# Forming the first modulation's shift and scale inside the input product's stage

## The reference, cut to what matters

```python
c_act = jax.nn.silu(c)                                   # c: (1, 1024)
mod = c_act @ w_ada[l] + b_ada[l]                        # w_ada: (1024, 6*1024)
shift1, scale1, gate1, shift2, scale2, gate2 = jnp.split(mod, 6)
h = layer_norm(x) * (1.0 + scale1) + shift1              # x: (1024, 1024)
proj = h @ w_in[l]                                       # w_in: (1024, 6416)
```

## Time and profile before

| | |
|---|---|
| Median of 3 runs | 4945.96 us (4945.6 to 4948.31) |
| The profiled execution's own time | 4957.9 us |
| Its span in the trace | 4956.0 us |
| PE busy | 4270.7 us (86%) |
| DVE, ACT, POOL busy | 53%, 31%, 15% |
| Moved by DMA | 589.38 MB, mean 119 GB/s |

### The profile page before, as it was taken

The page is one execution under the profiler, slowest core; times in us unless marked ns, Lnnn a source line. Parts: engine busy times, 40 slices in busy tenths (PEclk is TensorE's granted clock), DMA queues, the critical chain, the costliest instruction groups (busy, mean ns, idle before and its releaser), DMA issues. The chain is left out here.

```text
span 4956.0 us, 70950 instructions
## 1 busy us (share of the span) xinstructions
PE 4270.7 (86%) x27114; PEld 3547.5 (72%) x27114; DVE 2633.8 (53%) x4845; ACT 1526.3 (31%) x3235; POOL 741.6 (15%) x796
## 2 busy tenths in 40 slices
PE   5999999866999999699967576999985799989978
PEld 3899888555788877599966133888874699965646
DVE  3557774655343358411107696777754425546745
ACT  3233221633222235211114242334433411133423
POOL 1111111221000000000004012111112114423321
PEclk8999999777999999799988588999986899999998
DMA  4544432531211144322121484434424335543334
GB/s 158 165 141 139 146 127 78 195 138 60 59 51 42 34 153 166 102 86 86 65 107 49 165 299 158 105 98 112 108 65 132 124 106 173 182 147 101 100 98 136
DMA packets 430680, 589.38 MB, mean 119 GB/s; under 512 B 166297, under 2 KB 317201, under 8 KB 428771
## 3 DMA queue, kind: packets, MB, share of 16 engines
q1 hardware_dynamic: 382425, 418.41, 27.6%
q0 software_dynamic: 46336, 164.57, 8.9%
q10 hardware_dynamic: 1616, 2.36, 0.1%
HBM read 429.67 MB, written 155.57 MB: 118 GB/s over the span
## 5 line engine op out<-in xcount | busy, mean ns | idle before, releaser
L320 PE MATMUL g_in_g_acc<-g_in_g_whi,g_in_hi 128*128 128x444 f32 (+4 forms) x960 | 357.0, 372 | 16.6 <-DVE g_in_g_wlo L310 9.9
L321 PE MATMUL g_in_g_acc<-g_in_g_wlo,g_in_hi 128*128 128x444 f32 (+4 forms) x960 | 346.3, 361 | 0.0
L322 PE MATMUL g_in_g_acc<-g_in_g_whi,g_in_lo 128*128 128x444 f32 (+4 forms) x960 | 345.7, 360 | 0.0
L196 PE MATMUL g_even_acc<-g_even_w_hi,h_hi 128*128 128x384 f32 (+1 forms) x960 | 317.3, 331 | 19.5 <-DVE g_even_w_lo L238 19.5
L198 PE MATMUL g_even_acc<-g_even_w_lo,h_hi 128*128 128x384 f32 (+1 forms) x960 | 317.1, 330 | 0.0
L199 PE MATMUL g_even_acc<-g_even_w_hi,h_lo 128*128 128x384 f32 (+1 forms) x960 | 317.1, 330 | 0.0
L320 PE MATMUL g_odd_g_acc<-g_odd_g_whi,h_hi 128*128 128x344 f32 (+3 forms) x816 | 263.9, 323 | 31.9 <-DVE g_odd_g_wlo L310 16.8
L321 PE MATMUL g_odd_g_acc<-g_odd_g_wlo,h_hi 128*128 128x344 f32 (+3 forms) x816 | 261.8, 321 | 0.0
L322 PE MATMUL g_odd_g_acc<-g_odd_g_whi,h_lo 128*128 128x344 f32 (+3 forms) x816 | 261.7, 321 | 0.0
L1597 DVE SCALAR_TENSOR_TENSOR up_cv<-up_acc,up_taps,up_cv 128x1023 f32<-128x1023 f32 x88 | 112.8, 1282 | 279.7 <-ACT up_cv L1573 272.5
L214 DVE COPY g_even_o_buf<-g_even_acc 128x384 f32<-128x384 f32 (+1 forms) x60 | 32.1, 535 | 399.2 <-PE g_even_acc L199 399.2
(11 more groups left out here) (582 smaller groups left out, 10357.3 us busy)
## 6 DMA issues: line engine op xcount, KB each, us to landing
down_raw<-in_w_down SPq DMA_DIRECT2D x66, 512.0 KB
g_in_m_w<-in_ada_w SPq DMA_DIRECT2D x24, 1024.0 KB, 5.7
up_w_buf<-in_w_up SPq DMA_DIRECT2D x44, 512.0 KB
U2p<-g_even_o_buf POOLq DMA_DIRECT2D x11, 1920.0 KB, 7.8
g_odd_x<-U3p SPq DMA_DIRECT2D x24, 768.0 KB
g_even_w_buf<-in_even_w_in SPq DMA_DIRECT2D x11, 1536.0 KB
g_in_m_w<-in_w_ada SPq DMA_DIRECT2D x16, 1024.0 KB, 6.1
prep_near<-U2p SPq DMA_DIRECT2D x18, 896.0 KB
```

What stands on the lines that cost most here:

```text
L196: mm = pe.matmul(o, hi[:, k, tt], w_hi[:, par, k, :wd], start=k == 0, stop=not split and k == kc - 1)
L320: pe.matmul(bank[:, :wd], hi[:, k, tt], w_hi[:, st % 2, k, :wd], start=k == 0, stop=False)
L321: pe.matmul(bank[:, :wd], hi[:, k, tt], w_lo[:, st % 2, k, :wd], start=False, stop=False)
L322: op = pe.matmul(bank[:, :wd], lo[:, k, tt], w_hi[:, st % 2, k, :wd], start=False, stop=k == KC - 1)
```

## The change

`start_stage` and `ada_stage` go. `in_stage` takes their work:

- The first weights are loaded by SP at the head of its queue into `first_w`, in 8 transfers of 1 MB (four strips of 512 columns, each in two halves), with the loads of the first four chunks of `w_in` between the second and the third strip. `first_w` lies in the memory that `hi` and `lo` take later.
- ACT issues the loads of `c`, of the bias as 16 rows and of `ident`, takes silu, and issues the four writes of zero rows. The first reader of the padded tensors' stage is guarded by `pad_out` in `load_x`.
- PE transposes the bias rows (into `bias_T`), then forms the modulation as columns: the weights are the stationary operand (128 rows by 64 columns), one column of `c_first` is the moving one, and the two halves of 64 columns go to partitions 0 to 63 and 64 to 127. That is 64 such products for a strip, 256 in all: strips 0 and 1 ahead of the transposes of block 0, strips 2 and 3 behind them.
- DVE copies the turned bias to `cols` ahead of norm(0), and adds the sums to it in turn_in(0).

```diff
+FIRST = 4
-        start_stage(nc, ident, T["t_eye"], (U2p, U3p))
-        ada_stage(nc, [([T["c"][0]], T["w_ada"][0][:, 0:2 * D], T["b_ada"][0][0:2 * D], mod1[:, 0:2 * D])])
...
+        with nc.sbuf_tensor("g_in_first", [P, FIRST, KC, 512], F32) as first_w:
+            pass
         hi = sb("hi", [P, KC, SEQ], F32R)
         lo = sb("lo", [P, KC, SEQ], F32R)
...
+        half = lambda h: slice(h * (KC // 2), (h + 1) * (KC // 2))
+        sums_of = pm[:].rearrange("p a c -> p (a c)")[:, 0:2 * KC]
+        bias_T = pS[:, 0, 0:2 * KC]
+        zeros = x[:, 0, 0:P]
...
         @block.sync
+            def load_first(n):
+                for h in range(2):
+                    sp.dma_start(first_w[:, n, half(h)], w_first.rearrange("(p k) n -> p k n", k=KC)[:, half(h), n * 512:(n + 1) * 512]).then_inc(first_in[2 * n + h], DMA)
+
             def load_x(t):
+                if t == 0:
+                    sp.wait_ge(s.pad_out, 2 * len(padded) * DMA)
...
-            sp.dma_start(shift_scale_rows[:], shift_scale.rearrange("(r p) -> r p", p=P)).then_inc(s.rows_in, DMA)
-            for c in range(KC + RAW):
+            for n in range(FIRST):
+                load_first(n)
+                if n == FIRST // 2 - 1:
+                    for c in range(RAW):
+                        gemm.load(sp, c)
+            for c in range(RAW, KC + RAW):
                 gemm.load(sp, c)
...
+            def column_sums(n):
+                for h in range(2):
+                    pe.wait_ge(first_in[2 * n + h], DMA)
+                for c in range(4):
+                    for k in range(KC):
+                        for g in range(2):
+                            e = slice(g * 64, (g + 1) * 64)
+                            op = pe.matmul(sums_of[e, 4 * n + c:4 * n + c + 1], first_w[:, n, k, c * P + g * 64:c * P + (g + 1) * 64], c_first[:, k], start=k == 0, stop=k == KC - 1)
+                if n == FIRST - 1:
+                    op.then_inc(s.cols_T, 1)
+
             def turn_in(t):
+                if t == 0:
+                    pe.wait_ge(s.id_in, DMA)
+                    pe.wait_ge(s.rows_in, DMA)
+                    pe.transpose(bias_T, bias_rows[:], ident[:2 * KC, :2 * KC]).then_inc(s.bias_T, 1)
+                    pe.wait_ge(s.c_silu, 1)
+                    for n in range(FIRST // 2):
+                        column_sums(n)
                 pe.wait_ge(s.xn, t + 1)
...
                 op.then_inc(s.in_T, 1)
+                if t == 0:
+                    for n in range(FIRST // 2, FIRST):
+                        column_sums(n)
...
         @block.scalar
+            act.dma_start(c_first[:], conds[0].rearrange("(p k a) -> p k a", k=KC, a=1), allow_slow_non_contiguous=True).then_inc(s.c_in, DMA)
+            act.dma_start(bias_rows[:], b_first.rearrange("(r p) -> r p", p=P)).then_inc(s.rows_in, DMA)
+            act.dma_start(ident[:], t_eye).then_inc(s.id_in, DMA)
+            act.wait_ge(s.c_in, DMA)
+            act.activation(c_first[:], c_first[:], ACT.Silu).then_inc(s.c_silu, 1)
+            act.wait_ge(s.zero, 1)
+            for t in padded:
+                for row in (0, t.shape[0] - 1):
+                    act.dma_start(t[row].rearrange("(q c) -> q c", c=P), zeros[0:t.shape[1] // P]).then_inc(s.pad_out, DMA)
...
                     dve.wait_ge(s.cols_T, 1)
-                    flat = pm[:].rearrange("p a c -> p (a c)")
-                    dve.tensor_copy(cols[:, 0:KC], flat[:, 0:KC])
-                    dve.tensor_scalar(cols[:, KC:], flat[:, KC:2 * KC], 1.0, None, ALU.add)
+                    dve.tensor_tensor(cols[:, 0:KC], sums_of[:, 0:KC], cols[:, 0:KC], ALU.add)
+                    dve.scalar_tensor_tensor(cols[:, KC:], sums_of[:, KC:], 1.0, cols[:, KC:], ALU.add, ALU.add)
...
             def first(t):
+                if t == 0:
+                    dve.memset(zeros, 0.0).then_inc(s.zero, 1)
+                    dve.wait_ge(s.bias_T, 1)
+                    dve.tensor_copy(cols[:], bias_T)
                 norm(t)
```

More of the change, by code:

```diff
@@ L57, in col_view @@
     return vec.rearrange("(k p) -> p k", p=P)
[L60 to L119, removed]
@@ L1031, with in_stage @@
 SWA_FROM = QB_STRIPS * NT
-def in_stage(nc, ident, src, shift_scale, w_in, P1, pos, sinks, t_mask, t_first, t_freq, YB, conds, mods):
-    with stage(nc, "g_in", "cond", "silu", "rows_in", "cols_T", "cols", "in_even", "in_odd", "var", "std", "xn", "in_T", "h", "h_hi", "h_lo",
+def in_stage(nc, ident, t_eye, padded, src, w_first, b_first, w_in, P1, pos, sinks, t_mask, t_first, t_freq, YB, conds, mods):
+    with stage(nc, "g_in", "id_in", "zero", "pad_out", "c_in", "c_silu", "f0", "f1", "f2", "f3", "f4", "f5", "f6", "f7", "bias_T", "cond", "silu", "rows_in", "cols_T", "cols", "in_even", "in_odd", "var", "std", "xn", "in_T", "h", "h_hi", "h_lo",
                "m_even", "m_odd", "mb0", "mb1", "mb2", "mb3", "m_acc", "m_mm", "m_res", "m_out_even", "m_out_odd", "const", "init", "arg", "table", "x_even", "x_odd", "roped", "turned", "qkT", "scores", "s_free",
@@ L1072, in in_stage @@
         y = sb("y", [P, SH, SHD])
-        shift_scale_rows = sb("shift_scale_rows", [2 * KC, P])
+        bias_rows = sb("bias_rows", [2 * KC, P])
+        c_first = sb("c_first", [P, KC, 1])
         cols = sb("cols", [P, 2 * KC])
@@ L1091, in in_stage @@
         xn, h = pT[:, 0].rearrange("p c t -> p (c t)"), pT[:, 1]
+        first_in = (s.f0, s.f1, s.f2, s.f3, s.f4, s.f5, s.f6, s.f7)
+        half = lambda h: slice(h * (KC // 2), (h + 1) * (KC // 2))
+        sums_of = pm[:].rearrange("p a c -> p (a c)")[:, 0:2 * KC]
+        bias_T = pS[:, 0, 0:2 * KC]
+        zeros = x[:, 0, 0:P]
         def in_order(norm, turn_in, unit, step, mod):
@@ L1250, in step @@
                     score(t, n // 2)
-            def turn_in(t):
+            def column_sums(n):
[8 more added lines that the diff above has]
+                    op.then_inc(s.cols_T, 1)
+            def turn_in(t):
+                if t == 0:
[5 more added lines that the diff above has]
+                        column_sums(n)
                 pe.wait_ge(s.xn, t + 1)
[L1254 to L1257, removed]
+                if t:
                     pe.wait_ge(s.h, t)
@@ L4023, in tables @@
     }
[L4026 to L4043, removed]
 @contextmanager
@@ L4082, in program @@
     with nc.sbuf_tensor("ident", [P, P], F32) as ident:
-        start_stage(nc, ident, T["t_eye"], (U2p, U3p))
-        ada_stage(nc, [([T["c"][0]], T["w_ada"][0][:, 0:2 * D], T["b_ada"][0][0:2 * D], mod1[:, 0:2 * D])])
         rest = [((0,), T["w_ada"][0][:, c:c + MOD_W], T["b_ada"][0][c:c + MOD_W], mod1[:, c:c + MOD_W]) for c in range(2 * D, 6 * D, MOD_W)]
         rest += [((1, 2), T["ada_w_2"][n][:, c:c + MOD_W], T["ada_b_2"][n][c:c + MOD_W], mod2[n][:, c:c + MOD_W]) for n in range(2) for c in range(0, 3 * D, MOD_W)]
-        in_stage(nc, ident, x, mod1[0, 0:2 * D], T["w_in"][0], P1, T["positions"][0], T["swa_sinks"][0], T["t_mask"], T["t_first"], T["t_freq"], YB,
+        in_stage(nc, ident, T["t_eye"], (U2p, U3p), x, T["w_ada"][0][:, 0:2 * D], T["b_ada"][0][0:2 * D], T["w_in"][0], P1, T["positions"][0], T["swa_sinks"][0], T["t_mask"], T["t_first"], T["t_freq"], YB,
                  [T["c"][0], T["c_2"][0], T["c_ctx_2"]], rest)
```

## The result

| | before | after |
|---|---|---|
| Median | 4947.14 us (6 runs, 4944.6 to 4958.86) | 4919.97 us (6 runs, 4918.72 to 4934.02) |
| Profiled execution, span | 4956.0 us | 4919.4 us |
| Unit 0 starts on PE | 82.56 us | 51.23 us |

The ratio is 0.9944, 95% interval 0.9933 to 0.9955: 27.7 us less, with 22 to 33 in the interval. The change made the kernel faster, by less than the 36.6 us of the forecast; the median lies 6 us above the likeliest case's own range (4905 to 4914) and 1 us inside the upper end of the wide one (4904 to 4921). That upper end was drawn to take in part of a slow stream, not for what happened, so the hit is in part luck.

What follows compares the result with a forecast made beforehand. Opening latencies in a row were taken to delay unit 0; moving it from 82.56 to 46.0 us saves 36.6, so 4957.9 becomes 4921.3, less 11.9 from profile to median: 4909.4 us, 8-in-10 range 4904 to 4921.

Steps and rivals of the forecast that it cites:

- the likeliest case's own range: Main forecast for the whole kernel: 4909.4 us, own range 4905 to 4914, chance 0.80.
- the column sums: PE's modulation products ahead of unit 0: 28 to 56 ns a pair, 1.8 to 3.6 us a strip, done at 38.5 to 40.3.
- the sign of an error: Opening weight stream: the forecast called itself wrong if PE is busy through the island, meaning the pairs are dear.
- The cover: Column sums under the weight transfers: 1.8 to 3.6 us of sums hide under 5.7 us of transfer per strip.
- Start of the stream: First weights on SP's queue: issue at 0.9 us, data from 3.1, strip 0 ready for PE at 14.3.
- Rate: Opening weight stream: 367 GB/s, so 11.8 MB take 32.2 us and the last weights have moved at 35.3.
- The late request: SP's request for chunk 4 of `w_in`, waiting for chunk 0's split: at 28.4 us, 5 us ahead of the weights' end, costing nothing.
- What follows unit 0: Units behind unit 0: order unchanged, chunk 8 still in time, so the whole shift of 36.6 us passes on.
- idle slices between the islands: Gaps between bursts of weight transfers in the old opening: given 16 of the 36.6 us gain.
- Slow stream: Rival: opening transfers run at 254 GB/s or a small load is late; unit 0 at 61.3, 4924.8 us; chance 0.10.
- Loads and products in turn: Rival: in the column sums loads and products do not overlap, 365 ns a pair; unit 0 at 115.5, 4979 us; chance 0.05.
- A pair between 94 and 236 ns: Rival: column-sum pairs slowed as by a column's write-back; at 165 ns unit 0 at 64.3, 4928 us; chance 0.03.

Runs made afterwards that it cites:

- The run with half the sums: Changed kernel with every second chunk of the contraction left out of the column sums, same transfers; one execution 4923.77 us, unit 0 at 46.84.
- the run with 64 columns: Changed kernel with 64 equal columns as moving operand of the column sums instead of one; one execution 4910.2 us, unit 0 at 48.20.
- the second profile: Another profiled execution of the changed kernel, nothing altered; unit 0 at 50.97 us, last product of the input stage at 822.3.
- the run with a warm PE: Changed kernel with 24 unused products of 512 columns ahead of PE's first own work; one execution 4929.77 us, unit 0 at 58.93.
- the middle way: Changed kernel with 64 equal columns, third token block asked for after the third strip lands, POOL's other later loads after the last; 4911.04 us, ratio 0.9931.

## Why the prediction came out as it did

**The step that failed: the column sums.** I took 28 ns on the higher clock and 56 on the lower for a "pair" and gave a strip 64 of them, 1.8 to 3.6 us. The 24 weight loads of the earlier trace rows are passes, not products: that loop issues 12 products of float32. A strip is 128 passes at 54.6 ns and measured 6.99 us. The distance at the lower clock was right, the number of steps was half of what runs. The clue was in my own rows: before the change the program issues 8 products for a strip, and the timeline shows x16. The consequence is the one that I had named as the sign of an error: 6.99 us is more than the 5.7 us of a strip's transfer, so PE stays busy through the island and becomes the bound. Sums and transposes are 4 x 6.99 + 1.97 = 29.9 us from 14.59 on, with a wait of 1.22 us for strip 1 in between; they end at 45.4 (31.61 + 13.82), where I had 38.5 to 40.3. Unit 0 is 5.2 us late: 1.6 us of that lie in the splits (41.9 instead of 40.3) and 3.6 in the sums that end behind them. The run with half the sums shows this directly.

**The cover was mis-sized, the mechanism not.** "PE keeps up and only the last strip lies on the path" is what the run with 64 columns shows at the higher clock (strip 3 waits 0.47 us for its data).

**Start of the stream: right.** First issue at 0.88, strip 0 on PE at 14.59 (forecast 14.3, without the dent). **Rate: right in the mean, with a dent.** From 2.85 to 38.5 us the slices average 352 GB/s (forecast 367), with most of them at 360 to 410 outside 10 to 16 us, where POOL's loads took about 2.3 us of stream (four slices that moved 258, 334, 139 and 188 instead of some 385). Hence strip 3 at 38.3 instead of 36.7 (in the run with 64 columns) and chunk 7 split at 41.9 instead of 40.3. The late request is not the reason: with 64 columns chunk 4 was asked for at 29.08 and chunk 7 was split at 41.9 as well (40.8 with half the sums). The stream alone would have put unit 0 at 41.9 + 0.3 + 5.4 = 47.6.

**The late request, the bias, Silu and the zero rows: right in kind.** Chunk 4 is asked for at 33.28, 4.9 us behind the forecast of 28.4 since it waits for the dear sums, but with strips still landing; DVE copies the bias at 10.48 and no engine waits for these beyond.

**What follows unit 0: right, as far as the traces tell.** 31.3 us at unit 0 and 30.4 at the end of the input products; 31.6 and 33.7 in the second profile.

**A share that was miscounted.** The forecast gives 16 us to idle slices between the islands. In the earlier trace rows the 8.39 MB take from 13.3 to 45.8 us, 32.5 us, where 22.9 would do at 367 GB/s, so 9.6 us are idle there; 16 comes near only with the empty slices behind the last island. No term of the sum rests on it.

**From the trace to the median.** 10.6 us lie between 4909.4 and 4919.97. The late unit 0 is 5.2 of them, 3.6 by the sums and 1.6 by the stream; the median of before moved by 1.2 (4945.96 to 4947.14). The other 4.2 are the difference between the 31.3 us seen at unit 0 and 27.2 between medians; that is inside the interval of 22 to 33, and no cause was looked for.

**The rivals.** *Slow stream* gave 4924.8, near the result, but for another reason: the stream ran at its full rate outside the dent. *Loads and products in turn* is refuted: loads of 227 ns and matmuls of 245 start every 53 ns. The Trainium skill, "TensorE: Matmul & The Clock Gate", section "Part 3: Packing small matmuls — row/col tiling", lists that a load overlaps products in flight only where row groups differ; that does not describe this stream, in which every pass uses all 128 rows. The same section also lets a load go ahead into a background weight buffer; no run here shows whether that is what happens. *A pair between 94 and 236 ns* is, by its price, what happened: 109 ns a product. But its reason, a column that must be written back, is not what was seen: the same passes start 30 ns apart at the higher clock, and 64 columns cost the same 54 ns as one at the lower. It was given 0.03 because the 28 ns seemed to be measured on the same form.

## What to carry to other kernels

Before a row's distance is taken as the price of an instruction, count the rows against the program's instructions: a float32 product here leaves two loads and two matmuls, at twice the price of one. When a transfer is meant to hide work, compare the work per piece at the lower clock with the transfer per piece. Transfers that nobody needs yet are best asked for behind the stream that sets the end, but not so late that their own reader waits; the timelines here show both sides, the times between these runs do not settle it.

## What the runs showed of the hardware

One-column passes without a gap fell to the lower clock while they ran (granted 0.97, then 0.50, in the run with a warm PE), and in the changed kernel 13.82 us of them stayed at 54.6 ns a pass. With 64 equal columns the clock rose in the middle of a strip, and a pass cost no more; in the middle way it also fell again in the midst of such a strip, 1 us behind a wait of 3.64 us. On the DMA side POOL's loads of some 60 KB in small pieces and two masks of 128 KB came with a loss of 40% of the rate of the stream on SP's queue (a mean of 230 GB/s instead of 385) over four slices, 5.7 us; the loss was there without the third token block and gone with all these loads late. Why loads so small cost so much was not settled.
